# Five RMS norms whose square sums move from TensorE to GpSimd

## The reference

```python
def rms_norm(x, w):
    xf = x.astype(jnp.float32)
    y = xf * lax.rsqrt(jnp.mean(xf * xf, axis=-1, keepdims=True) + EPS)
    return (y * w.astype(jnp.float32)).astype(x.dtype)

for l in range(DEPTH):                                    # first part
    h_lat = rms_norm(x, norm_pre_mix[l]) * (1.0 + sc1) + sh1
    ...
    x = x + g1 * rms_norm(y_lat, norm_post_mix[l])        # a norm,
    h_lat = rms_norm(x, norm_pre_ffn[l]) * (1.0 + sc2) + sh2   # and a norm right behind it
    x = x + g2 * rms_norm(conv_ffn(h_lat, ...), norm_post_ffn[l])
...
return rmsnorm(x, final_norm_g)                           # end of the second part
```

## Time and profile before

| | us |
|---|---|
| median of 3 runs | 3538.64 (3533.36 to 3541.53) |
| profiled execution, span of its instructions | 3526.8 |
| PE busy | 3386.2 (96%) |
| DVE busy | 865.3 (25%) |
| ACT busy | 690.6 (20%) |
| POOL busy | 92.7 (3%) |

### The profile page before, as it was taken

One profiled execution on the slowest core, in us unless ns is written; L12 is line 12 of the kernel. 1 busy time (PEld: TensorE's weight loads), 2 busy tenths in 40 slices (PEclk: granted clock), 3 DMA queues, 4 the chain that ended last, 5 costly groups with the idle time before them and its releaser, 6 DMA issues.

```text
span 3526.8 us, 79917 instructions
## 1 busy us (share of the span) xinstructions
PE 3386.2 (96%) x34474; PEld 2825.9 (80%) x34475; DVE 865.3 (25%) x1982; ACT 690.6 (20%) x1496; POOL 92.7 (3%) x141
## 2 busy tenths in 40 slices
PE   8999699999999999999999999989999999999998
PEld 4456658884557788787799887779999999988898
DVE  1114636650102321214265113220100010011000
ACT  2224122221113421212211112211111111111011
POOL 0000000110001000100000010000000000000000
PEclk9999689999899999999999999989999999999999
DMA  6546012222223244343344443349999999944376
GB/s 275 179 155 230 13 48 84 84 72 77 83 85 117 98 151 138 128 143 104 121 146 156 142 143 109 108 146 368 375 352 351 368 378 345 372 158 153 137 284 259
DMA packets 94771, 637.72 MB, mean 181 GB/s; under 512 B 10785, under 2 KB 11825, under 8 KB 38593
## 3 DMA queue, kind: packets, MB, share of 16 engines
q1 hardware_dynamic: 92048, 627.58, 49.1%
q0 software_dynamic: 2608, 8.49, 0.7%
HBM read 634.98 MB, written 1.05 MB: 180 GB/s over the span
## 4 chain that ended last, share of the span: by engine, by line
PE 93%; DVE 3%; DMA 2%; ACT 2%; issue 1%; SPq 0%; ACTq 0%; DVEq 0%
PE bank L949 20%; PE bank L528 20%; PE bank L621 18%; PE bank L571 11%; PE bank L642 5%; PE bank L542 4%; PE bank L909 2%; PE bank L476 2%; PE bank L502 1%; PE bank L678 1%; PE bank L964 1%; DMA ring<-in_moe_down 1%; PE bank L660 1%; PE bank L667 1%; PE bank L1017 1%
## 5 line engine op out<-in xcount | busy, mean ns | idle before, releaser
L621 PE MATMUL bank<-PROJ,ring 128*64 128x96 f32 (+2 forms) x7776 | 663.8, 282 | 1.7 <-DMA ring<-in_moe_down 1.0
L621 PEld LDWEIGHTS bank<-PROJ,ring 128*64 128x64 f32 (+1 forms) x7776 | 545.6, 147 | 118.0 <-issue 85.4
L528 PE MATMUL bank<-H,ring 128*128 128x256 f32 (+1 forms) x2336 | 619.4, 426 | 5.9 <-ACT H L1125 5.9
L528 PEld LDWEIGHTS bank<-H,ring 128*128 128x128 f32 x2336 | 444.6, 191 | 164.6 <-issue 111.0
L949 PE MATMUL bank<-MIX,ring 128*64 128x96 f32 x12544 | 519.3, 246 | 7.9 <-issue 7.7
L949 PEld LDWEIGHTS bank<-MIX,ring 128*64 128x64 f32 x12544 | 517.8, 137 | 9.9 <-issue 9.8
L949 PE MATMUL bank<-H,ring 128*128 128x256 f32 x896 | 193.7, 379 | 0.0
L949 PEld LDWEIGHTS bank<-H,ring 128*128 128x128 f32 x896 | 170.2, 190 | 23.4 <-issue 0.3
L642 PE MATMUL bank<-H,ring 128*128 128x256 f32 x768 | 177.9, 389 | 3.9 <-ACT PROJ L1196 3.7
L1892 DVE TENSOR_TENSOR PROJ<-SC,bank 128x96 f32 (+1 forms) x224 | 61.7, 275 | 475.5 <-ACT SC L1323 471.3
L642 PEld LDWEIGHTS bank<-H,ring 128*128 128x128 f32 x768 | 147.8, 195 | 28.1 <-issue 7.7
(11 more groups left out here) (318 smaller groups left out, 3010.1 us busy)
## 6 DMA issues: line engine op xcount, KB each, us to landing
ring<-in_moe_up SPq DMA_DIRECT2D x224, 1024.0 KB, 5.0
ring<-in_moe_down SPq DMA_DIRECT2D x128, 896.0 KB, 6.1
ring<-in_up SPq DMA_DIRECT2D x44, 1024.0 KB, 4.8
ring<-in_mod_b SPq DMA_DIRECT2D x40, 1024.0 KB, 5.1
ring<-in_tproj SPq DMA_DIRECT2D x32, 1024.0 KB, 4.8
ring<-in_proj SPq DMA_DIRECT2D x26, 1024.0 KB, 4.9
ring<-in_gates SPq DMA_DIRECT2D x24, 1024.0 KB, 4.8
ring<-in_down SPq DMA_DIRECT2D x32, 704.0 KB, 4.0
```

What stands on the lines that cost most here:

```text
L528: mm = pe.matmul(B[(tile + t) % 4][:, 0:width], w[:, k, t * P:(t + 1) * P], src[:, k, 0:width], start=k == 0, stop=k == k_n - 1)
L621: mm = pe.matmul(B[bank][lo:lo + m, 0:width], w[:, k, lo:lo + m], src(s * half + k), start=s == 0 and k == 0, stop=s == 1 and k == half - 1)
```

## The change

In norms 2, 4, 6, 8 and 12 GpSimd now adds square tiles 1 to 6 onto tile 0 (`square_sums`), each addition behind its square and behind the one before. TensorE waits for the whole sum, takes its means, and then those of tile 7. The per-norm semaphores of the squares become one that counts on, and a new one, `norm_pacc`, counts GpSimd's sums. GpSimd's wait ahead of the bias transfers of layer 1 is replaced by its part in norm 4.

```diff
+POOLED = (2, 4, 6, 8, 12)
...
-                if summed:
-                    pe.wait_ge(S("norm_acc"), summed)
-                    means(0, True, False)
-                    pe.wait_ge(S(f"norm{n}_sq"), KT)
-                    means(KT - 1, False, True).then_inc(S("norm_ms"), 1)
-                else:
-                    for k in range(KT):
-                        pe.wait_ge(S(f"norm{n}_sq"), k + 1)
-                        mm = means(k, k == 0, k == KT - 1)
-                    mm.then_inc(S("norm_ms"), 1)
+                pe.wait_ge(S("norm_acc" if summed else "norm_pacc"), summed or 1 + POOLED.index(n))
+                means(0, True, False)
+                pe.wait_ge(S("norm_sq"), KT * n + KT)
+                means(KT - 1, False, True).then_inc(S("norm_ms"), 1)
...
+            def square_sums(n, width):
+
+                for k in range(1, KT - 1):
+                    pool.wait_ge(S("norm_sq"), KT * n + k + 1)
+                    ins = pool.tensor_tensor(H[:, 0, 0:width], H[:, 0, 0:width], H[:, k, 0:width], ALU.add)
+                    if k < KT - 2:
+                        step(ins)
+                    else:
+                        ins.then_inc(S("norm_pacc"), 1)
...
+            square_sums(2, TC)
             conv_ffn(0, TC)
-            pool.wait_ge(S("norm_ms"), 4)
+            square_sums(4, TC)
             for v in range(2, 2 * C_HEADS):
...
+            square_sums(6, T)
             conv_ffn(1, T)
+            square_sums(8, T)
             for l in range(DEPTH):
                 window_means(l)
+            square_sums(12, T)
```

More of the change, by code:

```diff
@@ L1108, in squares @@
                     act.wait_ge(sem, first + every * k)
-                    act.activation(H[:, k, 0:width], src[:, k, 0:width], ACT.Square).then_inc(S(f"norm{n}_sq"), 1)
+                    act.activation(H[:, k, 0:width], src[:, k, 0:width], ACT.Square).then_inc(S("norm_sq"), 1)
             def root(n, width):
@@ L1132, in take_tile @@
             def take_tile(n, k, bank, row, width):
-                act.activation(H[:, k, 0:width], bank[:, 0:width], ACT.Square).then_inc(S(f"norm{n}_sq"), 1)
+                act.activation(H[:, k, 0:width], bank[:, 0:width], ACT.Square).then_inc(S("norm_sq"), 1)
                 for s in range(width // T):
@@ L1481, in sum_square @@
             def sum_square(n, k, width):
-                dve.wait_ge(S(f"norm{n}_sq"), k + 1)
+                dve.wait_ge(S("norm_sq"), KT * n + k + 1)
                 ins = dve.tensor_tensor(H[:, 0, 0:width], H[:, 0, 0:width], H[:, k, 0:width], ALU.add)
```

## The result

| | before | changed |
|---|---|---|
| median of 20 runs, us | 3532.01 (3525.39 to 3541.53) | 3543.09 (3536.75 to 3548.64) |
| span of the profiled execution, us | 3526.8 | 3546.8 |

The ratio is 1.0029, with an interval of 1.0022 to 1.0036: the changed kernel is slower by about 10 us (7.8 to 12.7). The profiled execution of the changed kernel is the slowest of its 20 (3548.64 us, 1.8 more than its span), so its span is not to be set against that of before as a whole. The lengths of single stages can be.

What follows compares the result with a forecast made beforehand. It took TensorE as the bound (93% of the chain), its means at half clock. Norms 2, 4, 6, 8 and 12 gave 2.6 + 1.5 + 1.15 + 1.7 + 0.5 = +7.45 us on 3538.64, so 3546.1, range 3537 to 3552.

Steps and rivals of the forecast that it cites:

- The turns: Norms 2, 4, 6, 8: GpSimd additions and VectorE two-SBUF-input operations alternate, 1.78 or 0.97 us per tile; +2.6, +1.5, +1.15, +1.7 us.
- Rival A: Norms 2, 4, 6, 8: no turns with two-input additions, 1.34 us a tile; -0.6 us, 3538.0; chance 0.15.
- Rival B: Norms 2, 4, 6, 8: longer holds, periods of 2.03 and 1.22 us, `w_sums` slip too; +13 us, 3551.6; chance 0.11.
- Rival C: Norm 2: VectorE always wins, GpSimd's fifth and sixth additions wait for `w_sums`; +6.8 there, +11.7 in all, 3550.3; chance 0.06.
- The step from the copies: Hold sizes taken from GpSimd copies in the recurrence: a 512-column addition holds the way 1.18 us, a 256-column one 0.64.
- Norm 12: VectorE idle, so GpSimd's additions come every 0.80 us; the means end at 3516.97 instead of 3516.49: +0.5 us.
- The 11.8 us "around the span": Time outside the profiled span of 3526.8 us, added to the new span of 3534.3 us to give the forecast time.
- the edits put at nothing: Renamed semaphore, GpSimd's additions ahead of its products, and later bias transfers of layer 1: no cost.
- The late bias transfers: First two bias transfers of layer 1 start some 15 us later, covered by 150 us before their first user: no cost.

Runs made afterwards that it cites:

- e3_psum: Changed kernel, but VectorE's scaled tile goes to a PSUM bank, so the sum has one SBUF and one PSUM operand; 3535.31 us, ratio 1.0015 to before.
- e7_late: Changed kernel, but GpSimd starts its additions only when all eight squares of a norm are there; 3559.89 us in one run.
- e8: The kernel before once more, nothing changed, for a second trace; 3529.03 us in one run.
- e2_null: Changed kernel with its counting semaphore, but GpSimd adds in no norm and TensorE takes all eight tiles; 3534.16 us, ratio 1.0006 to before.
- e6: Changed kernel, but GpSimd adds only tile 6 onto 5 (norm 12: tiles 4 to 7), plus 4, 4, 2, 2 constant products in norms 2, 4, 6, 8; 3531.68 us, 0.9994.
- The split: Changed kernel, but GpSimd adds only tile 6 onto tile 5 (tiles 4 to 7 in norm 12), TensorE takes the others; 3533.3 us, ratio 1.0004 to before.
- e5_pad: Changed kernel plus 24, 24, 12 and 12 products of constants on TensorE in norms 2, 4, 6 and 8; 3537.21 us, ratio 1.0016 to before.

## Why the prediction was right, and where it was off

**The turns.** Right, down to the place. L1508 beside an addition takes 1.16 ("near 1.2"), additions start 1.68 us apart in norms 2 and 4 ("1.7 to 1.8", taken as 1.78) and 0.80 in norm 12, means take 3.57 at PEclk 0.50 ("3.5"), and the reciprocal of norm 2 stands right behind the last of `w_sums`. Rival A (period under 1.4) falls by e3_psum and e7_late, which show its 1.34 only where VectorE has no two SBUF operands. Rival B (2.03) falls by the 1.68. Rival C (VectorE always first) falls by GpSimd's last addition in norm 2, which ends at 509.08 + 9.96 = 519.04, beside the first operation of `w_sums` and 4.3 us ahead of the last.

**Their size.** The step from the copies was somewhat too dear: an addition of 512 columns holds VectorE out for 1.68 - 0.60 = 1.08 us, not 1.18, and in norms 6 and 8 additions come (5.06 - 0.73) / 5 = 0.87 apart, not 0.97. So norms 2, 4, 6 and 8 cost 1.95 + 1.00 + 0.69 + 1.25 = 4.9 us where I had 2.6 + 1.5 + 1.15 + 1.7 = 6.95.

**Norm 12.** Mis-sized the other way: +0.5 predicted, about +2.4 measured. I took the 6.43 us for 32 rows as what this place costs. It is one outcome of several. Here the means follow TensorE's work at once and may run at full clock (3.75 us); idling behind GpSimd takes that chance away, and GpSimd's chain is the longer one then.

**The sum.** 4.9 + 2.4 + 3.1 = 10.4 us, against the measured 10 (7.8 to 12.7). The predicted +7.45 was near because two errors, -2.05 in the turns and +5.0 in the two other terms, partly offset each other. That was luck, and so was the time: 3546.1 lies 3.0 over the measured 3543.09, but it stood on three runs of before whose median was 6.6 over that of twenty. The 11.8 us "around the span" were mostly that too: an execution takes some 1.8 us more than its span (3548.64 against 3546.8, and 3529.03 against 3527.2 in e8). Of the edits put at nothing the semaphore was nothing (e2_null). The late bias transfers, issued at 966.50 in the changed kernel, were covered: their first user still waits for TensorE (timeline of VectorE, changed kernel).

```profile
1121.65 0.69 DVE L1556 CUSTOM_DVE_ANT_0 SC<-bank,PROJ 128x512 f32<-128x512 f32 x1 [143.86 <-PE bank L657]
```

**What the profiles differ by beyond that.** The spans are 20 us apart. 1.9 us of it is there at 444 us, ahead of everything changed; about 2.7 us appears between 1551 and 1630, 3.1 between norms 9 and 11 and 3.1 behind the entry, where no line differs. Traces of one and the same kernel also differ by such steps, in stretches at half clock that fall differently, and before itself runs from 3525 to 3542. Only terms that repeat over several traces are counted above.

**Open.** The NOPs have a rule now; the branch has none. With 16 NOPs it took 0.48 to 0.72 us in five traces and 3.50 in e6; with 48, 2.92 to 3.56; with 64, 1.64 and 1.66; with 224, 2.50 and 2.52. In each of the eleven traces where it takes more than 0.48 us it ends 1.4 to 1.5 us after a packet of the instruction queue (q8, 16384 bytes) has landed. The packet starts at 2358.6 in before, 2.1 us ahead of the branch, and at 2362.0 in e6, 1.0 us behind the branch's start. That reads as a wait for instructions, but no run moves the packet by itself, so it is argued, and why it comes late in e6 stays open. Open too is what brings the half-clock stretches between norms 9 and 11. No version is shown to beat the kernel before. The split saves 3.8 us in its norms, but no variant of it had the entry of before.

## What to carry to other kernels

Before GpSimd is given work beside VectorE, look at which VectorE operations on the path have two SBUF operands: here each GpSimd addition of 1.27 us cost 1.08 us on that path, and one operand in PSUM removed it. Take over only as much as the slower engine can finish before the last input arrives: in these norms one addition gained and six, taking turns, lost (the gain isn't shown in the time). When a few instructions come or go, look at every aligned loop behind them as well. Count the NOPs of its `addr_align` and the length of its first branch in the views of those lines, since the wait that the timeline puts down to nothing can move by more than the change is worth.

## What was not expected of the hardware

- The entry of an aligned loop on TensorE cost 2.8 to 16.6 us here. Its alignment consists of 16 to 224 NOPs, one every 0.073 us; 12 products of one column, placed over 1800 us earlier, made 208 more of them and 13.6 us of difference.
- The first branch of that loop took 0.48 to 3.56 us, and 3.50 in a kernel with as many products ahead of it as one where it took 0.48.
- The granted clock did not rise while TensorE was busy without a pause with products of one column. In e5_pad, with the constant products in norm 2, PE is busy for 2.00 of 2.00 us and PEclk stays at 0.50:

```profile
508.00:510.00 2.00, 2.00 (x11) 2.00 (x11) 2.00 (x3) 0.95 (x2) 1.92 (x2) 0.50 0.00 0
```

- GpSimd's additions and VectorE's operations with two SBUF operands took turns, one each, in norms 2, 4, 6 and 8: 1.68 us a pair with 512 columns and 0.87 with 256. The hold of 1.08 us is 0.19 less than the addition's own 1.27 us. The rule of the whole instruction is stated on the page "SBUF — State Buffer" of the Trainium skill, in "Who interferes with whom" for VectorE's two-port modes and in "Summary: rules for kernel authors" for two SBUF inputs as well. For two plain SBUF operands the trace gives this somewhat shorter hold.
